# FFN gate and up pairs as seven half products: 19 pairs instead of 13, three lower parts of each made on GpSimd

## The reference, cut to what matters

```
h = x * (1.0 + sc2) + sh2                       # 512 x 1024
gu = h @ w_ffn_in                               # 1024 x 5632
f = (silu(gu[..., :2816]) * gu[..., 2816:]) @ w_ffn_out
x = layer_norm(ALPHA * x + gt2 * f, ln2_g, ln2_b)
```

## Time and profile before

| | |
|---|---|
| runs | 1573.64, 1573.38, 1569.16 us |
| profiled execution | 1572.88 us; its span on the core is 1570.8 us |
| busy, share of the span | PE 1518.1 us (97%), PEld 80%, DVE 1093.5 (70%), ACT 749.5 (48%), POOL 191.9 (12%) |
| chain that ended last | PE 79%, DVE 15%, ACT 3% |
| granted TensorE clock | 0.995 of full on average |
| weight loads | 289 of 512 KB, median 3.5 us from issue to landing |

### The profile page before, as it was taken

How to read it: one execution, slowest core, us unless ns; L and a number is a source line. 1 busy time by engine, 2 the same in 40 slices (tenths; PEclk the granted TensorE clock), 3 DMA queues, 4 the chain that set the end, 5 groups by cost and what they waited for, 6 DMA issues and landing times.

```text
span 1570.8 us, 25892 instructions
## 1 busy us (share of the span) xinstructions
PE 1518.1 (97%) x10408; PEld 1252.6 (80%) x10408; DVE 1093.5 (70%) x1898; ACT 749.5 (48%) x1253; POOL 191.9 (12%) x159
## 2 busy tenths in 40 slices
PE   7999999999999999999999999988898999999998
PEld 6878786888888877777788888767767899989886
DVE  5999994666655478758544747886547978867556
ACT  5544455535522477747632625654424544444223
POOL 2435364500010000000004000000000000000000
PEclk9999999999999999999999999999999999999999
DMA  6323243454465323232424232210002233433331
GB/s 220 94 86 120 90 147 108 160 165 146 147 184 182 116 86 95 90 111 81 147 95 142 74 121 81 81 43 4 3 29 86 90 108 106 123 97 121 101 98 54
DMA packets 45798, 166.18 MB, mean 106 GB/s; under 512 B 5280, under 2 KB 5408, under 8 KB 45680
## 3 DMA queue, kind: packets, MB, share of 16 engines
q1 hardware_dynamic: 43056, 155.95, 30.8%
q0 software_dynamic: 2624, 8.59, 1.9%
HBM read 162.42 MB, written 2.10 MB: 105 GB/s over the span
## 4 chain that ended last, share of the span: by engine, by line
PE 79%; DVE 15%; ACT 3%; issue 2%; DMA 0%; SPq 0%; DVEq 0%; ACTq 0%
PE bank L643 24%; PE bank L645 24%; PE bank L644 23%; DVE bank L2390 7%; PE bank L1366 1%; PE bank L1218 1%; ACT scratch L654 1%; DVE small L2416 1%; DVE x_rows L2390 1%; PE bank L1197 1%; DVE scratch L2387 0%; DVE weight_lo L699 0%; PE bank L1463 0%; ACT weight_hi L691 0%; DMA x_in<-in_x 0%
## 5 line engine op out<-in xcount | busy, mean ns | idle before, releaser
L691 ACT ACTIVATE weight_hi<-raw 128x1024 fp32r<-128x1024 f32 x195 | 205.8, 1057 | 384.6 <-PE bank L645 381.1
L643 PE MATMUL bank<-h_T_hi,weight_hi 128*128 128x512 f32 (+1 forms) x848 | 342.0, 403 | 2.8 <-DVE conv_in L2387 2.1
L699 DVE TENSOR_TENSOR weight_lo<-raw,weight_hi 128x1024 fp32r<-128x1024 f32 x138 | 168.8, 1224 | 238.6 <-ACT weight_hi L691 238.6
L645 PE MATMUL bank<-h_T_hi,weight_lo 128*128 128x512 f32 (+1 forms) x848 | 329.8, 389 | 0.0
L644 PE MATMUL bank<-h_T_lo,weight_hi 128*128 128x512 f32 (+1 forms) x848 | 329.2, 388 | 0.0
L643 PEld LDWEIGHTS bank<-h_T_hi,weight_hi 128*128 128x128 f32 x848 | 160.1, 189 | 43.2 <-issue 8.5
L2390 DVE SCALAR_TENSOR_TENSOR bank<-conv_in,columns,bank 128x512 f32<-128x512 f32 x240 | 181.4, 756 | 8.3
L644 PEld LDWEIGHTS bank<-h_T_lo,weight_hi 128*128 128x128 f32 x848 | 160.3, 189 | 33.5 <-issue 3.6
L645 PEld LDWEIGHTS bank<-h_T_hi,weight_lo 128*128 128x128 f32 x848 | 159.8, 188 | 33.8
L699 POOL TENSOR_TENSOR weight_lo<-raw,weight_hi 128x1024 fp32r<-128x1024 f32 x57 | 141.8, 2488 | 154.1 <-ACT weight_hi L691 154.1
L643 PE MATMUL bank<-h_T_hi,half_weight_hi 128*128 128x256 f32 (+1 forms) x240 | 79.1, 330 | 0.0
(11 more groups left out here) (500 smaller groups left out, 3193.0 us busy)
## 6 DMA issues: line engine op xcount, KB each, us to landing
raw<-in_weights SPq DMA_DIRECT2D x289, 512.0 KB, 3.5
x_in<-in_x SPq DMA_DIRECT2D x4, 512.0 KB, 5.8
x_rows<-in_x POOLq DMA_DIRECT2D x4, 512.0 KB, 4.9
out<-x_rows SPq DMA_DIRECT2D x3, 512.0 KB, 2.6
mem_in<-in_mem POOLq DMA_DIRECT2D x2, 512.0 KB, 4.2
ln_rows<-in_ln_g POOLq DMA_DIRECT2D x4, 256.0 KB, 4.4
ln_rows<-in_ln_b POOLq DMA_DIRECT2D x4, 256.0 KB, 5.1
silu_row<-in_c POOLq DMA_DIRECT2D x1, 512.0 KB, 6.6
```

The lines of the kernel that those rows point to most:

```text
L643: pe.matmul(o, lhs[0], rhs[0], start=start, stop=False, skip_group_check=onto)
L645: return pe.matmul(o, lhs[1], rhs[0], start=False, stop=stop, skip_group_check=onto)
L691: act.activation(weight_parts(u)[0][:, :], raw[u % RAW][:, :], ACT.Copy).then_inc(*weight_hi.up(u))
L699: engine.tensor_tensor(lo[:, :], raw[u % RAW][:, :], view(hi[:, :]), ALU.subtract).then_inc(*ready.up(u))
```

## The change

Pairs 3, 6, 9, 12, 15 and 18 become sevens too, so that `SEVENS` is every pair from 2 to 20. For each seven the lower parts of B11, B21 and B22 are made by GpSimd, in that order, with a semaphore of their own (`part_lo_pool`); T1 to T4 stay on DVE. SP and PE wait for whichever engine makes the part. The gain rows stay in pairs 5, 8, 11 and 14, and GpSimd loads the last norm rows after the parts of pair 16.

```diff
-SEVENS = tuple(n for n in range(2, FT) if n % 3)
+SEVENS = tuple(range(2, FT - 1))
+POOL_PARTS = ("B11", "B21", "B22")
+GAINS_AT = (5, 8, 11, 14)
+LAST_ROWS_AT = 16
...
-                        sp.wait_ge(*part_lo.at(n, "B21" if label == "ffn_g" else "B22"))
+                        sp.wait_ge(*part_ready(n, "B21" if label == "ffn_g" else "B22"))
...
-        pool.wait_ge(*moved.at("ln1", TT - 1, 1))
-        norm_rows("ln2")
+        for n in SEVENS:
+            for part in POOL_PARTS:
+                rest_of_part(pool, n, part, part_lo_pool)
+            if n == LAST_ROWS_AT:
+                pool.wait_ge(*moved.at("ln1", TT - 1, 1))
+                norm_rows("ln2")
...
-            pe.wait_ge(*part_lo.at(n, part))
+            pe.wait_ge(*part_ready(n, part))
...
+    def part_ready(n, part):
+        return part_lo_pool.at(n, part) if n in SEVENS and part in POOL_PARTS else part_lo.at(n, part)
+
+    def rest_of_part(engine, n, part, ready):
+        hi, lo = half_of(n, part)
+        engine.wait_ge(*part_hi.at(n, part))
+        engine.tensor_tensor(lo, part_source(n, part), view(hi), ALU.subtract).then_inc(*ready.up(n, part))
...
-                dve_part(dve, n, part)
+                if n not in SEVENS or part not in POOL_PARTS:
+                    rest_of_part(dve, n, part, part_lo)
...
-        if n + 1 not in SEVENS and n > SEVENS[0]:
+        if n in GAINS_AT:
             dve_gains(dve)
```

More of the change, by code:

```diff
@@ L628, in build @@
     weight_summed, part_hi, part_lo = signal("weight_summed"), signal("part_hi"), signal("part_lo")
+    part_lo_pool = signal("part_lo_pool")
     used, seven_act, seven_dve = signal("part_used"), signal("seven_act"), signal("seven_dve")
@@ L3106, in dve_sum @@
         dve_rest(dve, sums[name][1][:, :, :], full_sums[name][:, :, :], sums[name][0][:, :, :], sum_hi.at(name)).then_inc(*sum_lo.up(name))
-    def dve_part(dve, n, part):
-        hi, lo = half_of(n, part)
-        dve_rest(dve, lo, part_source(n, part), hi, part_hi.at(n, part)).then_inc(*part_lo.up(n, part))
     def dve_parts(dve, n, first, last):
```

## The result

The changed kernel takes 1614.57 us (median of 4 runs, 1613.36 to 1615.93), the kernel before in the same session 1572.32 us (4 runs, 1569.16 to 1573.64). The ratio is 1.0271, with a 95% interval of 1.0256 to 1.0286: 42.2 us slower where 30 were forecast. The profiled execution took 1613.36 us, its span is 1611.6 us. Of the lines named here, L647 to L649 are the matmuls (before L643 to L645), L2311 the lower part of a weight part on either engine, L3142 the differences, L3174 the bank additions, L2403 the product, L658 ACT's silu, L2324 its high parts.

The account below looks back on a forecast made before the run. PE was taken as the bound with DVE close behind; after the change DVE's loop would bound. From 1572.88 us, -10.1 + 27.4 + 10.6 + 1 + 1 = +29.9 gave 1603 us, range 1578 to 1614, chance 0.80.

Parts of the forecast that it names:

- PE, six pairs shorter: Six whole pairs become sevens on PE, from 11.20 to 9.52 us each: 10.1 us less if PE stays the bound.
- the lock: SBUF port shared by DVE and GpSimd: each GpSimd subtraction closes it to DVE's two-SBUF-operand operations for 1.16 us.
- The loop is then 8.36 + 2.8 = 11.15: DVE's loop in a seven, 8.36 us plus 2.8 of port waits, exceeds PE's 9.52; 17 x 1.6 = 27.4 us more.
- gain rows: Pairs 5, 8, 11, 14: DVE's 2.66 us each, before hidden by a whole pair, now count fully; 10.6 us more.
- diagonals in pair 17: Eight DVE operations of 1.65 us in all enter the loop in pair 17; 0 to 1.65, taken as 1 us.
- entry into pair 2: Pair 2, where DVE comes late from the token sums; by the diagonals' bounds, 1 us more.
- Rivals 1 and 2: 1: port holds lightly, 1570 us, chance 0.09; 2: no port wait, gain rows absorbed, 1563 us, chance 0.07.
- rival 1: GpSimd's reads close the port for 0.4 us, PE bounds, gain rows cost 6.2; 1570 us, up to 1577, chance 0.09.
- Rival 3: Wholly serial: every GpSimd operation adds its full 1.31 us, nothing lies under an addition; 1622 us, chance 0.04.
- own upper bound of 1610: The upper ends of the forecast's own terms taken together, 1610 us; its lowest own case was 1591.

## Why the prediction came out as it did

Direction and mechanism hold, and the marks named in the last part of the prediction appear: PE waits for ACT's silu, pairs of 11.4 us and of 14.1 with gain rows, DVE operations of up to 1.8 us. Only GpSimd's subtractions stayed at 1.84 us at most, where over 2 were named. The size fell short: +42.2 us against +29.9, and 1614.57 us lies 0.6 above the range. Step by step, from the pairs of the profiled execution:

| step of the prediction | forecast, us | measured, us | from |
|---|---|---|---|
| PE, six pairs shorter | -10.1 | -10.1 | a seven without the lock is 9.52 |
| "The loop is then 8.36 + 2.8 = 11.15" | 17 x 1.6 = +27.4 | 16 x 1.9 + 3.0 = +33.4 | pairs 2 to 17, and 18 to 20 |
| gain rows | +10.6 | +10.6 (11.0 by the run without them, where the clock changed too) | pairs 5, 8, 11, 14 |
| diagonals in pair 17 | +1 | +3.5 | 17.65 us, less the loop and the 2.7 of before |
| entry into pair 2 | +1 | +2.4 | 14.11 us |
| (no term) half clock | 0 | +1.4 | pairs 12, 15 |
| sum | +29.9 | +41.2 | stage: 257.6 - 216.3 = 41.3 |

**The loop.** The base is right: 11.42 less the measured 3.0 us of lock is 8.4 (forecast 8.36), and DVE alone gives 10.39 (forecast 10.2; the other 0.19 is DVE's wait for B21's high part, 0.79 us from T4's lower part to B21's instead of 0.60, which the kernel before has too). The step that was mis-sized is "B22 and B11 come due while DVE has the product and three differences back to back. Each either slips between two of them (1.16 us) or gets in under an addition", of which I took the middle, 2.8. The timeline of pair 4 shows that GpSimd gets in after every single DVE operation as long as it has one waiting; neither of the two finds an addition to hide under (B21's does begin under one, and costs the 0.8 us of the forecast). It was the upper end in every pair from 3 to 16 but 12 and 15, where the product took 0.91 and 0.85 us only and PE, at half clock, set the time. 0.27 us a pair is small, but PE had no slack left, so it came in full in the others.

That the excess reaches PE through bank 0 was right. The end of pair 4 (C22 on DVE and PE's B22, then C21 on DVE, silu, T4's high part, silu of C11, PE) reads:

```profile
1272.46 0.41 DVE L3174 TENSOR_TENSOR scratch<-scratch,bank 128x256 f32<-128x256 f32 x1
...
1272.92 0.39 PE L647 MATMUL bank<-sum_S_hi,half_weight_hi 128*128 128x256 f32 x1 [0.79 <-DVE scratch L3174]
...
1273.39 0.41 DVE L3174 TENSOR_TENSOR scratch<-scratch,bank 128x256 f32<-128x256 f32 x1
1273.83 0.42 ACT L658 ACTIVATE scratch<-scratch 128x256 f32<-128x256 f32 x1 [2.06 <-DVE scratch L3174]
1274.16 0.61 ACT L2324 ACTIVATE half_weight_hi<-weight_sum_T 128x512 fp32r<-128x512 f32 x1
1274.68 0.36 ACT L658 ACTIVATE scratch<-bank 128x256 f32<-128x256 f32 x1
...
1275.09 0.38 PE L647 MATMUL bank<-h_T_hi,half_weight_hi 128*128 128x256 f32 x1 [0.53 <-ACT scratch L658]
```

C21 starts 9.7 us into the pair and PE 1.7 us after it; the prediction had 7.8 us as the point from which PE waits, and 1.66 us from C21 to PE. It did not have the wait ahead of it, 0.79 us at B22 until C22 had read bank 4, so that only 0.53 of the 1.3 us are waited at bank 0. By the order of the times the earlier wait costs nothing of its own, since bank 0 came free later still; no run takes it away alone.

The count was one short as well: pair 17 was taken as free beside its gate rows and has the loop's excess too. Pairs 18 to 20, with no gain rows and a whole pair behind, cost 3.0 together where two of them stood for 3.2.

**The diagonals.** The eight operations were taken at their usual 1.65 us. Pair 17, the operations behind the product of pair 16:

```profile
1435.87 3.68 DVE L3074 TENSOR_SCALAR scratch<-ident,mod 128x128 f32<-128x128 f32 x8
...
1436.09 2.60 POOL L2311 TENSOR_TENSOR half_weight_lo<-raw,half_weight_hi 128x512 fp32r<-128x512 f32 x2 [6.71 <-ACT half_weight_hi L2324]
...
1438.91 1.10 PE L1581 MATMUL bank<-scratch,ones_all 128*128 128x512 f32 x2 [3.89 <-DVE scratch L3074]
```

They took 3.68 us, two of them 1.29 and 1.30 instead of 0.27, and PE waited 3.89 us for them ahead of the gate rows. My bound, 0 to 1.65, had left the lock out of this step, and it had left out that PE was waiting there.

**The clock.** No term stood for it. Windows of the end of pair 5, of the next two stretches, and of pair 11 into 12:

```profile
1285.90:1289.17 3.27, 0.12 (x3) 0.01 (x1) 2.23 (x5) 1.26 (x4) 0.00 (x0) 1.00 0.00 0
1290.10:1293.50 3.40, 3.40 (x18) 3.40 (x17) 3.40 (x3) 0.96 (x3) 3.40 (x3) 0.50 0.39 104
1293.60:1300.60 7.00, 7.00 (x62) 7.00 (x61) 6.00 (x11) 3.07 (x7) 0.79 (x1) 1.00 0.30 96
1361.80:1368.60 6.80, 5.63 (x26) 5.64 (x27) 5.79 (x6) 3.05 (x7) 4.62 (x3) 0.50 0.36 91
```

PE stood still for 3.15 us at the end of a gain pair, and 0.9 us later the granted clock is at half, the 1.2 GHz level, for 3.4 us. It came four times in the stretch (twice for 6.8 us), which the kernel before doesn't show there. DVE set the time there, so most of it was hidden in pair 6, which lasted 11.52 us. Pair 15 lasted 12.74 and pair 12 12.26, of which pair 13 (10.70) gave 0.7 back. The same gap behind pair 8 (3.19 us) was followed by no half clock; with all lower parts on DVE each of the four (3.14 to 3.19 us) was, and with writes in place of reads, where the gaps are 1.33 us, none was. A gap that a wait makes can so cost a second time.

**The rivals.** Rivals 1 and 2 needed a light or absent lock; the run with writes in place of reads is rival 1 made true, and gives 1572.72 us for its 1570 to 1577. Rival 3 (1622 us) had nothing hidden under an addition, 1.31 us for each; measured are 0.84, 1.10 and 1.10. Of its two halves the first, nothing under an addition, is what happened for B22 and B11. Its chance of 0.04 was low for that: the true time lies between it and the forecast. My own upper bound of 1610 had the 1.16 us for both and 1.65 for the diagonals; what was missing above it are the clock, the lock in pair 17 and the entry.

## What to carry to other kernels

Before work is moved from VectorE to GpSimd, count what VectorE has with two SBUF operands near it: here 0.60 us of relief cost 0.76 to 1.10 us of waiting each time. VectorE's operations with a bank operand were free of it, and those with two SBUF operands were free of GpSimd's writes; the diagonals, with one, were held up by both. Where both engines have a queue, reckon that they alternate after every instruction. When an engine close to the bound is asked for more, look first for its own standing waits: the order of two steps gave 12 us here, where GpSimd's help cost 21 to 23.

## What the runs showed of the hardware that was not expected

- An operation with one SBUF tensor operand was blocked too: the diagonals, 128x128, 1.29 and 1.30 us instead of 0.27 while GpSimd subtracted. The Trainium skill (SBUF — State Buffer, section "SBUF: two separate sides") names, beside operations with two SBUF inputs, those in a two-port performance mode, and asks only of the former that GpSimd's operation read SBUF. The kernel with writes in place of reads agrees: the diagonals were held up there too (0.49 to 0.62 us), the operations with two SBUF inputs were not. That these eight ran in such a mode follows from this only by the Trainium skill; no trace names the mode.
- The step between matmuls has two values that no edit explains. In the kernel with the reordered T4, then in the one with the gate rows in halves (PE, start and us; six matmuls left out in each):

```profile
1285.88 0.28 PE L648 MATMUL bank<-h_T_lo,half_weight_hi 128*128 128x256 f32 x1
...
1286.70 0.28 PE L649 MATMUL bank<-sum_S_hi,half_weight_lo 128*128 128x256 f32 x1
```

```profile
1285.94 0.28 PE L647 MATMUL bank<-h_T_hi,half_weight_hi 128*128 128x256 f32 x1
...
1286.73 0.28 PE L648 MATMUL bank<-h_T_lo,half_weight_hi 128*128 128x256 f32 x1
```

Seven steps take 0.82 us in the one and 0.79 in the other, and over a pair of 84 matmuls 9.89 and 9.52 us (117.7 and 113.3 ns), with PE busy throughout and a granted clock of 1.00 in both. The code of pairs 3 to 16 is the same in both kernels. A stretch keeps its value for many pairs, but both values come in one execution too: in the kernel with the gate rows in halves pairs 3 to 17 have 113.3 ns and pairs 19 and 20 have 117.8. So the step can't be put down to the kernel, of which one trace each was taken. This is 5 us of such a stage, as much as the gain that is at stake, and its cause is open: no experiment here was made for it. It is also why the gain of the last kernels is read from their medians of ten or more runs and not from a stage length alone.
